# A two-layer decoder trunk on one core: three buffers for the old residual rows in the second layer's output projection, and bank waits at each bank's first use

## The reference

```python
h = rms_norm(res, pre_g[layer]) * (1.0 + scale[:, None, :]) + shift[:, None, :]
...
y, z, v_first = rwkv7_mixer(h, ...)
out = (y * jax.nn.silu(z)) @ rw_w_out[j]
...
res = res + gate[:, None, :] * rms_norm(out, post_g[layer])
```

## Time and profile before

| | us |
|---|---|
| median of three executions | 3538.35 |
| fastest, slowest of them | 3529.3, 3553.95 |
| profiled execution | 3545.52 |
| its span | 3543.7 |

### The profile page before, as it was taken

How to read it: one execution, slowest core, us unless ns; L and a number is a source line. 1 busy time by engine, 2 the same in 40 slices (tenths; PEclk the granted TensorE clock), 3 DMA queues, 4 the chain that set the end, 5 groups by cost and what they waited for, 6 DMA issues and landing times.

```text
span 3543.7 us, 80467 instructions
## 1 busy us (share of the span) xinstructions
PE 3286.5 (93%) x35338; PEld 1989.4 (56%) x35338; DVE 1604.9 (45%) x3443; ACT 1314.0 (37%) x2492; POOL 222.4 (6%) x345
## 2 busy tenths in 40 slices
PE   2899999999999968999999999999999999999998
PEld 1555465556455535666566466556466656556663
DVE  7245254435534544344564244554244454244442
ACT  0343344343434353333453133444133453223332
POOL 0010001010001000000000000000000000000000
PEclk8999999999999988999999999999999989999999
DMA  8231322331224131112112212112212112121111
GB/s 333 73 97 49 120 84 85 96 97 48 82 86 121 49 108 38 39 39 63 38 39 68 79 39 63 26 51 63 78 39 67 33 39 62 46 77 39 39 61 42
DMA packets 275862, 247.53 MB, mean 70 GB/s; under 512 B 16253, under 2 KB 251961, under 8 KB 272953
## 3 DMA queue, kind: packets, MB, share of 16 engines
q1 hardware_dynamic: 273208, 233.99, 21.0%
q0 software_dynamic: 2304, 8.39, 0.7%
HBM read 217.17 MB, written 25.18 MB: 68 GB/s over the span
## 4 chain that ended last, share of the span: by engine, by line
PE 75%; DVE 12%; DMA 5%; ACT 5%; issue 2%; SPq 1%; DVEq 0%; ACTq 0%; another core or an unknown queue 0%
PE bank L679 20%; PE bank L539 14%; PE bank L648 7%; PE bank L765 4%; PE bank L778 4%; PE bank L536 3%; PE bank L774 3%; DVE xm L1561 3%; PE bank L568 2%; DVE arena L1622 2%; PE bank L690 2%; DMA xm<-in_ada_w 2%; PE bank L820 1%; DMA arena<-residual_scratch 1%; DVE arena L1632 1%
## 5 line engine op out<-in xcount | busy, mean ns | idle before, releaser
L679 PE MATMUL bank<-xm,wring 128*128 128x512 f32 x2048 | 933.6, 604 | 0.8 <-ACT arena L1104 0.8
L679 PEld LDWEIGHTS bank<-xm,wring 128*128 128x128 f32 x2048 | 383.2, 192 | 474.8 <-issue 462.4
L539 PE MATMUL bank<-arena,wring 128*128 128x512 f32 x1280 | 580.0, 593 | 12.5 <-ACT xm L969 5.1
L539 PEld LDWEIGHTS bank<-arena,wring 128*128 128x128 f32 x1280 | 231.0, 190 | 256.7 <-issue 246.0
L648 PE MATMUL bank<-wring,yT 128*128 128x512 f32 x776 | 340.2, 599 | 16.7 <-DVE yT L1681 5.4
L648 PEld LDWEIGHTS bank<-wring,yT 128*128 128x128 f32 x776 | 148.1, 192 | 204.9 <-issue 188.6
L1150 ACT COPY arena<-bank 128x256 f32<-128x256 f32 x256 | 96.4, 377 | 440.3 <-PE bank L778 440.3
L1837 POOL COPY r_Q<-ident 128x512 f32<-128x512 f32 x160 | 98.1, 613 | 2017.4 <-PE bank L778 2015.5
L1662 DVE COPY arena<-bank 128x64 f32<-128x64 f32 x256 | 57.3, 224 | 348.6 <-PE bank L810 342.8
L778 PE MATMUL bank<-arena,r_Q 64*64 64x32 f32 x5120 | 201.8, 222 | 0.2 <-issue 0.2
L765 PE MATMUL bank<-arena 64*64 64x32 f32 x5120 | 191.4, 221 | 1.6 <-DVE arena L1646 1.1
(11 more groups left out here) (278 smaller groups left out, 5097.2 us busy)
## 6 DMA issues: line engine op xcount, KB each, us to landing
wring<-in_rw_w_rkvz SPq DMA_DIRECT2D x128, 512.0 KB, 3.9
wring<-in_ev_w_in SPq DMA_DIRECT2D x96, 512.0 KB, 5.2
xm<-in_ada_w SPq DMA_DIRECT2D x16, 1536.0 KB, 12.0
wring<-in_ev_w_out SPq DMA_DIRECT2D x32, 512.0 KB, 5.3
wring<-in_rw_w_out SPq DMA_DIRECT2D x32, 512.0 KB, 5.5
layer_input<-arena SPq DMA_DIRECT2D x4, 2052.0 KB, 7.7
wring<-layer_input SPq DMA_DIRECT2D x16, 513.0 KB, 7.2
xm<-in_x POOLq DMA_DIRECT2D x16, 512.0 KB, 5.3
```

What stands on the lines that cost most here:

```text
L539: mm = pe.matmul(pj[:, :], w[:, k, :], hT[:, k, 1:1 + TB], start=(k == 0), stop=(k == KC - 1))
L679: mm = pe.matmul(bank[1 if m == PROJ_Z else 0][:, :], w[:, k, :], xmv[MIX_OF[m]][:, k, :], start=(k == 0), stop=(k == KC - 1))
```

## The change

- **Buffers.** `r_rows` gives each tile a place: tiles 0 and 3 use `r_x1`, tiles 1 and 2 the two halves of `r_Gs[0]`, the mask buffer of even units. It is free in period 9, 17 and 25 (the chunks of an odd unit read `r_Gs[1]`) from the end of unit 8, 16, 24 until the masks of unit 10, 18, 26, which are written in the same period, after the residual. Each tile has a semaphore of its own for its read.
- **SyncE.** The reads of tiles 0, 1, 2 are issued first; those of 1 and 2 wait for `y_ready`, the last chunk of the unit that used the buffer. Then come tile 0's store, tile 3's read (after that store has landed), tile 1's store, the four weight loads, and the stores of tiles 2 and 3.
- **VectorE.** Before the masks of unit 10, 18, 26 it waits for the stores of tiles 1 and 2.
- **TensorE.** The waits for banks 4 and 5 stand before the projection's second group, those for 6 and 7 before its third. The variance no longer waits for all additions; the bonus sum waits for six, and the scores for all eight.

```diff
+        r_rows = [r_x1, r_Gs[0][:, 0:D], r_Gs[0][:, D:2 * D], r_x1]
...
             def old_rows(b, j):
-                sp.wait_ge(x_out[j - 1] if j else x_out[JT - 1], 16 * (b + 1 if j else b) + 16)
+                if j in (1, 2):
+                    sp.wait_ge(S["y_ready"], min(RP * (b + 1) + 1, NU - 1) * NCH)
+                else:
+                    sp.wait_ge(x_out[JT - 1 - j], 16 * (b + 1 if j else b) + 16)
                 sp.wait_ge(r_save[j], 16 * (b + 1))
-                sp.dma_start(r_x1, resid[b:b + 1][0][:, j * D:(j + 1) * D]).then_inc(S["r_load"], 16)
+                sp.dma_start(r_rows[j], resid[b:b + 1][0][:, j * D:(j + 1) * D]).then_inc(r_load[j], 16)
...
-                sp.dma_start(out_v[b:b + 1][0][:, j, :], r_x1).then_inc(x_out[j], 16)
+                sp.dma_start(out_v[b:b + 1][0][:, j, :], r_rows[j]).then_inc(x_out[j], 16)
...
                 if v > RP and v % RP == 1:
                     for j in range(JT - 1):
                         old_rows(b, j)
-                        if j < JT - 2:
-                            new_rows(b, j)
+                    new_rows(b, 0)
+                    old_rows(b, JT - 1)
+                    new_rows(b, 1)
                     weights(v + 1, PROJ_V)
...
                     new_rows(b, JT - 2)
-                    old_rows(b, JT - 1)
                     new_rows(b, JT - 1)
...
-            for j in range(JT):
+            for j in range(JT - 1):
                 old_rows(n_blocks - 1, j)
+            new_rows(n_blocks - 1, 0)
+            old_rows(n_blocks - 1, JT - 1)
+            for j in range(1, JT):
                 new_rows(n_blocks - 1, j)
...
+                    if l and not early and gi == 1:
+                        pe.wait_ge(S["ms_free"], turn(BANKM, "bk", RP * (b + 1) + 1) + 1)
+                        pe.wait_ge(S["v_tok"], RP * (b + 1) + 2)
+                    if l and not early and gi == 2:
+                        pe.wait_ge(S["bkt"], RP * (b + 1) + 2)
+                        pe.wait_ge(S["y_sb"], RP * (b + 1) + 1)
...
-                        pe.wait_ge(S["ms_free"], turn(BANKM, "bk", v) + 1)
-                        pe.wait_ge(S["v_tok"], v + 1)
-                        pe.wait_ge(S["bkt"], v + 1)
-                        pe.wait_ge(S["y_sb"], v)
                         out_proj(v // RP - 1, 1, early=False)
...
-                    if v > RP and v % RP == 1:
-                        pe.wait_ge(S["ob"], 8 * n_blocks + 8 * (v // RP))
                     if v:
                         variance(v - 1)
                     if inv:
+                        if v > RP and v % RP == 1:
+                            pe.wait_ge(S["ob"], 8 * n_blocks + 8 * (v // RP - 1) + 6)
                         bonus_sum(v + 1)
                         project(v + 1, PROJ_V, 5, 6)
+                        if v > RP and v % RP == 1:
+                            pe.wait_ge(S["ob"], 8 * n_blocks + 8 * (v // RP))
                         scores(v + 1)
...
-                        V.wait_ge(S["r_load"], (b * JT + j + 1) * 16)
+                        V.wait_ge(r_load[j], (b + 1) * 16)
...
-                        old = r_x1[:, hh] if l else xres[:, j, hh]
+                        old = r_rows[j][:, hh] if l else xres[:, j, hh]
...
+                if v > RP and v % RP == 2:
+                    V.wait_ge(x_out[1], 16 * (v // RP) + 16)
+                    V.wait_ge(x_out[2], 16 * (v // RP) + 16)
```

More of the change, by code:

```diff
@@ L271, in build @@
         names = """su_rows su_post su_iota su_tr su_param su_csig su_cond su_lbe su_acc su_accd su_mm
-        su_done passed own_dve own_act own_pool r_load h1 h1_save n_std n_xn n_tr n_ev_act n_ev_dve w2_in pw_in
+        su_done passed own_dve own_act own_pool h1 h1_save n_std n_xn n_tr n_ev_act n_ev_dve w2_in pw_in
         pw_free hp_ready hp_ev h_sig h_gate h_sp h_en h_enc h_l2 h_lsu h_k h_cum h_ec h_dif h_e h_z h_lv h_lvc h_dk h_ek
@@ L282, in build @@
         x_out = [ctx.enter_context(nc.semaphore(f"x_out{j}")) for j in range(JT)]
+        r_load = [ctx.enter_context(nc.semaphore(f"r_load{j}")) for j in range(JT)]
         r_save = [ctx.enter_context(nc.semaphore(f"r_save{j}")) for j in range(JT)]
```

## The result

| | before | changed |
|---|---|---|
| median of six executions, us | 3552.02 | 3516.61 |
| lowest to highest | 3529.3 to 3557.23 | 3508.18 to 3522.23 |
| span of the profiled execution | 3543.7 | 3517.8 |

The ratio is 0.9907, with a 95% interval from 0.9886 to 0.9928: 33 us less of 3552. A second measurement, of six more executions beside 23 of the kernel before, gave 0.9899 (0.9878 to 0.9919). Both are faster for certain; whether by over 1% they do not tell.

The account below looks back on a forecast made before the run. TensorE, with work in 93% of the span, was taken as the bound. Three blocks' 30.5 us plus 2.3 at the end gave 32.8 us off the 3538.35 us median, forecast 3505.5, range 3488 to 3524.

Parts of the forecast that it names:

- The reload goes: TensorE's wait for the residual's additions at the variance disappears in three blocks: 17.6 us gained, with 2.4 us of cover.
- The clock comes back: From variance to scores in three blocks, TensorE's clock stays up without the idle before: 7.7 us gained, bounds 0 to 7.7.
- The wait at the front goes: The output projection starts right behind the transposes, its first group waiting only for banks 0 to 3: 5.2 us over three blocks.
- What is added there: VectorE's masks wait for the stores of tiles 1 and 2: costed at nothing, with 4.6 us of cover.
- The end of the kernel: In the last block VectorE no longer stands idle for tile 3's reload: 2.3 us gained.
- The sum: 10.1 us per block, 30.5 us over three blocks, plus 2.3 us at the end: 32.8 us, 0.93% less.
- C: At the scores, the additions are still late and a wait replaces the reload: 3522 us; chance 0.08.
- E: Early reads of tiles 1 and 2 come no earlier, leaving only the front's 5.2 us: 3533 us; chance 0.03.
- A: Elsewhere in the kernel, two or three of six clock falls vanish: 10 us more gained, 3495 us; chance 0.13.
- B: Elsewhere in the kernel, two or three new clock falls appear: 10 us less gained, 3516 us; chance 0.09.
- D: Tile 2's store delays VectorE's masks in units 9, 17, 25, one for one beyond 4.6 us: 3549 us if 19 late; chance 0.03.

Follow-up runs that it names:

- The fill of the gap: Kernel before plus six unread matmuls ahead of the wait for the additions, in each of the three blocks; ratio 0.9997 (0.9979 to 1.0014).
- both fills: Kernel before plus unread matmuls: six ahead of the additions' wait (three blocks), eight in the seventh chunk of units 5, 13, 21; ratio 0.9968, 11 us.

## Why the prediction was right

The forecast was 3505.5 us, that is 32.8 us less; the median is 3516.61 beside a kernel before of 3552.02, 35.4 us less, and the ratio times 3552 gives 33 us (26 to 40). The absolute times differ since three more executions of the kernel before moved its median up by 13.7 us. The range up to 3524 held it. That 32.8 and 33 agree so closely is luck: the interval is 14 us wide. What carries the forecast is the stages, where each term can be read by itself. The prediction's "About 1% is what a measurement of this kernel can tell from no change" was too careful: the intervals are 0.2% to either side.

1. *"The reload goes"*: right. All three waits at the variance are gone; 0.33 us was left with the buffers alone. The cover at the scores is 2013.98 - 2011.76 = 2.2 us, where 2.4 was worked out. Nothing came late in its place.
2. *"The clock comes back"*: right in its place: 2.67 us from variance to scores in all three blocks. The fill of the gap shows the cause. Whether it stays over the whole kernel is less sure than I had it: the fill alone gained nothing measurable, both fills 11 of 17.7 us, the buffers alone 22 of the 28 us of their stages. With both parts in, nothing is seen to be taken back: the stages gave 35.1 us, and the two measurements 33 and 36. I took 7.7, the upper of my two bounds, since PE has no gap from there on; the falls far behind were in the text, but as scatter that evens out, not as something that takes back a part.
3. *"The wait at the front goes"*: right, 1.83, 1.55 and 1.83 us, with no idle left. Alone it gave 1.0 to 1.8 us per block more than that, nearly all by the clock.
4. *"What is added there"*: the cost of nothing was right, the working less so. The longest landing seen before was 5.4 us; tile 2's store took 6.5, behind four weight loads. The cover is 8.0 us, not 4.6, all the same, for I had left the loads at the time where they were. Counted from the transposes' end they ran from 48.0 us before and from 43.2 now: 1.8 us earlier with the projection, and 2.9 us earlier within it.
5. *"The end of the kernel"*: 2.3 expected, 2.5 in the profile and 2.4 with that part alone.
6. *The sum*: per block 10.2, 12.1 and 10.3 us where 10.1 was forecast for each. The excess in period 17 is a fall of the clock inside the projection of the kernel before, which took 56.7 us there and 55.0 elsewhere.

*The rivals.* C (a wait in place of the reload) did not come. E (reads no earlier) did not come either: the idle time for the scratch rows is gone. A and B (the clock elsewhere) are not seen in the medians. The falls at 1780 and 1863 are no case of B, since they lie ahead of the change; the three stretches behind the blocks sum to 1.0 us less than before. The prediction let each fall vanish or a new one appear as the program shifts in time; in the profiles their places in the program stay, and what varies is whether one comes. D had its place right and its price wrong: the step that failed in it is "one for one". Behind a gap of 7 us the clock cost about as much again as the gap, so that rival would have been worth about twice what I gave it.

## What to carry to other kernels

One buffer that is read, changed and stored makes a chain of store and reload; look for the one link of it that the bottleneck engine waits for, and give it another place to live, which may be a buffer that is idle only in that stage. Judge such a change by the stretch of its stage in the trace (62.00 us in all twelve blocks of the four runs that have this order), since two runs of the whole scatter by more than a part is worth. And count an idle stretch of TensorE of several microseconds longer than the idle time itself: in its stage it costs the low clock behind it too. The short ones here did not: the projection behind 1.83 us of idle ran at 1.00 in period 9, and so did the matmuls behind 0.33 us.

## What the runs showed of the hardware that was not expected

- The clock's price for an idle stretch is not a constant: 1.4 to 2.8 us behind 3.3 to 3.6 us of idle, 2.5 us behind 5.8 us of idle followed by large matmuls, up to 8.6 us behind 7.2 us of idle followed by the recurrence's small ones (0.59 over 21 us). The length of the gap and what follows it differ at once here, so no run tells which of them sets the price.
- Falls of the clock recur in the same places of the program, whatever was edited, but not in every execution: the window near 1785 is at 1.00 in the first profile and at 0.58 in the changed kernel's. One such place (2325 to 2345) keeps its fall with PE busy for all 20 us. The one at 2410 to 2425 stands in three profiles of twelve. What decides over it stays open.
- Filling idle time with unread matmuls raises the clock there and gains little over the whole: 11 us for some 33 us of idle time, nearly all of it filled, in the kernel before, and nothing measurable in the changed one.
- Much of the scatter between executions of one kernel goes with the clock: over the 68 executions of the kernel before in the experiments' rounds, the mean granted clock lay between 0.966 and 0.980 and the time between 3539 and 3565 us, the longer the lower the clock (correlation -0.71).
- A store of 512 KB that lands in 2.6 us on a quiet queue took 6.5 us right behind four weight loads.
